# Layer norm of a convolution on one core: the mean over 1024 channels from one running sum and the last tile, in place of eight products

## The reference, cut to what matters

```python
def layernorm(x, g, b):
    mu = jnp.mean(xf, axis=-1, keepdims=True)
    var = jnp.mean(jnp.square(xf - mu), axis=-1, keepdims=True)
    y = (xf - mu) * lax.rsqrt(var + LN_EPS)
    return y * g + b

def conformer_conv(h, w_pw1, b_pw1, w_dw, b_dw, ln_g, ln_b, w_pw2, b_pw2):
    u = h @ w_pw1 + b_pw1
    a, gate = jnp.split(u, 2, axis=-1)
    u = a * jax.nn.sigmoid(gate)
    u = conv(u, w_dw, 31 taps, causal, one filter per channel) + b_dw
    u = jax.nn.silu(layernorm(u, ln_g, ln_b))
    return u @ w_pw2 + b_pw2
```

## Time and profile before

| | us |
|---|---|
| median of 3 runs (2274.26 to 2274.81) | 2274.33 |
| the profiled execution, its own time | 2274.24 |
| its span, first to last instruction | 2272.5 |
| TensorE busy | 2247.5 (99%) |
| VectorE busy | 1306.0 (57%) |
| ScalarE busy | 931.6 (41%) |
| GpSimd busy | 375.7 (17%) |
| the stage of the convolution, first tap product to the mean's last product | 816.7 to 988.9 |

### The profile page before, as it was taken

One profiled execution on the slowest core, in us unless ns is written; L12 is line 12 of the kernel. 1 busy time (PEld: TensorE's weight loads), 2 busy tenths in 40 slices (PEclk: granted clock), 3 DMA queues, 4 the chain that ended last, 5 costly groups with the idle time before them and its releaser, 6 DMA issues.

```text
span 2272.5 us, 32983 instructions
## 1 busy us (share of the span) xinstructions
PE 2247.5 (99%) x11012; PEld 1829.9 (81%) x11012; DVE 1306.0 (57%) x1848; ACT 931.6 (41%) x1438; POOL 375.7 (17%) x296
## 2 busy tenths in 40 slices
PE   8999999999999999999999999999999999999998
PEld 6777778888888898878888888887777888888886
DVE  5557756643434758875564544576665656454455
ACT  6675645442324544553332222254544333222222
POOL 2021101201010446723040000040000304000003
PEclk9999999999999999999999999999999999999999
DMA  4222223333333434412123333332121212333332
GB/s 145 65 66 62 69 74 102 111 93 94 100 99 115 120 101 131 131 46 84 56 85 101 93 100 95 95 95 66 56 65 56 84 56 87 99 93 102 96 96 87
DMA packets 395617, 202.80 MB, mean 89 GB/s; under 512 B 13792, under 2 KB 393200, under 8 KB 395520
## 3 DMA queue, kind: packets, MB, share of 16 engines
q1 hardware_dynamic: 394672, 199.34, 29.9%
q0 software_dynamic: 848, 2.16, 0.3%
HBM read 198.84 MB, written 2.10 MB: 88 GB/s over the span
## 4 chain that ended last, share of the span: by engine, by line
PE 87%; issue 6%; DVE 2%; ACT 2%; POOL 1%; DMA 1%; DVEq 0%; SPq 0%; ACTq 0%; POOLq 0%
PE bank L1816 24%; PE bank L1818 24%; PE bank L1817 24%; PE bank L2201 3%; PE bank L2193 2%; PE bank L1796 2%; PE bank L2290 1%; PE bank L2267 1%; PE bank L2363 1%; PE bank L2399 1%; PE bank L2110 1%; PE bank L2112 1%; PE bank L2111 1%; DVE m_w_lo L1148 1%; POOL m_sb_softplus L558 0%
## 5 line engine op out<-in xcount | busy, mean ns | idle before, releaser
L621 ACT ACTIVATE m_w_hi<-m_raw 128x1024 fp32r<-128x1024 f32 x332 | 351.3, 1058 | 823.4 <-PE bank L1818 819.6
L1816 PE MATMUL bank<-m_h_hi,m_w_hi 128*128 128x512 f32 x1504 | 608.2, 404 | 2.9 <-DVE m_w_lo L1148 1.6
L1818 PE MATMUL bank<-m_h_hi,m_w_lo 128*128 128x512 f32 x1504 | 587.0, 390 | 0.0
L1817 PE MATMUL bank<-m_h_lo,m_w_hi 128*128 128x512 f32 x1504 | 586.3, 390 | 0.0
L1148 DVE TENSOR_TENSOR m_w_lo<-m_raw,m_w_hi 128x1024 fp32r<-128x1024 f32 x332 | 447.8, 1349 | 108.5 <-ACT m_w_hi L621 105.0
L1816 PEld LDWEIGHTS bank<-m_h_hi,m_w_hi 128*128 128x128 f32 x1504 | 282.7, 188 | 66.7 <-issue 4.7
L1818 PEld LDWEIGHTS bank<-m_h_hi,m_w_lo 128*128 128x128 f32 x1504 | 282.3, 188 | 60.3
L1817 PEld LDWEIGHTS bank<-m_h_lo,m_w_hi 128*128 128x128 f32 x1504 | 282.9, 188 | 55.5 <-issue 2.4
L1816 PE MATMUL bank<-m_f_hi,m_w_hi 128*128 128x512 f32 x688 | 268.8, 391 | 0.2 <-DVE m_w_lo L1148 0.2
L1818 PE MATMUL bank<-m_f_hi,m_w_lo 128*128 128x512 f32 x688 | 267.8, 389 | 0.0
L1817 PE MATMUL bank<-m_f_lo,m_w_hi 128*128 128x512 f32 x688 | 267.7, 389 | 0.0
(11 more groups left out here) (394 smaller groups left out, 3064.5 us busy)
## 6 DMA issues: line engine op xcount, KB each, us to landing
m_raw<-in_ff_w SPq DMA_DIRECT2D x256, 256.0 KB, 3.0
m_raw<-in_conv_pw_w SPq DMA_DIRECT2D x48, 256.0 KB, 3.8
m_raw<-in_w_in SPq DMA_DIRECT2D x47, 256.0 KB, 3.2
m_raw<-in_w_ffn_gate SPq DMA_DIRECT2D x44, 256.0 KB, 3.1
m_raw<-in_w_ffn_up SPq DMA_DIRECT2D x44, 256.0 KB, 3.1
m_raw<-in_w_ffn_down SPq DMA_DIRECT2D x40, 256.0 KB, 2.9
m_raw<-in_w_gate SPq DMA_DIRECT2D x32, 256.0 KB, 3.0
m_mem_w<-in_mem_wk SPq DMA_DIRECT2D x32, 256.0 KB, 3.0
```

The lines of the kernel that those rows point to most:

```text
L621: act.activation(WH[:, v % 2], RAW[:, v % 2], ACT.Copy).then_inc(s.w_hi, 1)
L1816: pe.matmul(o, high[:, r, k, :], hi, start=start, stop=False)
L1817: pe.matmul(o, high[:, r, k, :], lo, start=False, stop=False)
L1818: last = pe.matmul(o, low[:, r, k, :], hi, start=False, stop=stop)
```

## The change

GpSimd gets a new buffer `TILE_SUM` (128x512, fp32) and six additions. Ahead of the tap sums of tile m, for m = 2 to 7, it adds finished tile m-1 to the running sum (the first of the six adds tiles 0 and 1); it waits for `cv_tile` to be m there. This stands in place of the wait for `cv_tile` to be m-1 that its first tap addition had. TensorE's eight mean products, six of them in the steps, one ahead of `last_taps` and one behind the last memory group, become two behind that group: one of `MEAN` with `TILE_SUM`, one with tile 7.

```diff
+        TILE_SUM = at("conv_tile_sum", 110, [P, T])
...
+            def tile_sum(m):
+                pool.wait_ge(s.cv_tile, m + 1)
+                total = pool.tensor_tensor(TILE_SUM[:], CV[:, 0, :] if m == 1 else TILE_SUM[:], CV[:, m, :], ALU.add)
+                if m == KD - 2:
+                    total.then_inc(s.cv_sum, 1)
+
             for m in range(KD):
                 total = SUMS[m % 2][:]
+                if m >= 2:
+                    tile_sum(m - 1)
                 for j in range(1, SUM_TAPS if m < KD - 1 else SUM_TAPS_LAST):
-                    if j == 1 and m >= 2:
-                        pool.wait_ge(s.cv_tile, m - 1)
...
-            def conv_mean(m):
-
-                pe.wait_ge(s.cv_tile, m + 1)
-                first, last = isinstance(m, int) and m == 0, isinstance(m, int) and m == KD - 1
-                return pe.matmul(TR[:], MEAN, pick(CV, m), start=first, stop=last)
+            def conv_mean():
+
+                pe.wait_ge(s.cv_sum, 1)
+                pe.matmul(TR[:], MEAN, TILE_SUM[:], start=True, stop=False)
+                pe.wait_ge(s.cv_tile, KD)
+                pe.matmul(TR[:], MEAN, CV[:, KD - 1, :], start=False, stop=True).then_inc(s.ln_mean, 1)
...
                 mem_value(0, 1, m, q + 1, SBK[2])
-                if before is not None:
-                    conv_mean(before)
                 mem_key(1, 2, m, q + 2, SBK[3])
...
             mem_value(1, 3, 1, 27, SBK[1])
             mem_value(1, 0, KD, 28, SBK[2])
-            conv_mean(KD - 2)
             last_taps()
             mem_value(1, 1, KD, 29, SBK[3])
-            conv_mean(KD - 1).then_inc(s.ln_mean, 1)
+            conv_mean()
```

More of the change, by code:

```diff
@@ L2217, in last_taps, with conv_units @@
                 mm.then_inc(s.cv_pe, 1)
-            def conv_units(m, prev=None, before=None):
+            def conv_units(m, prev=None):
                 if prev is None:
@@ L2238, in _ @@
             conv_units(1, 0)
-            conv_units(2, 1, 0)
+            conv_units(2, 1)
             with U.loop(pe, KD - 3, 2) as i:
-                conv_units(i + 3, i + 2, i + 1)
+                conv_units(i + 3, i + 2)
             mem_value(1, 3, 1, 27, SBK[1])
             mem_value(1, 0, KD, 28, SBK[2])
-            conv_mean(KD - 2)
             last_taps()
             mem_value(1, 1, KD, 29, SBK[3])
-            conv_mean(KD - 1).then_inc(s.ln_mean, 1)
+            conv_mean()
             for k in range(KD):
```

## The result

The changed kernel takes 2278.35 us (median of 16 runs, 2277.34 to 2279.82) against 2274.36 for the kernel before beside it (16 runs, 2274.01 to 2274.89). The ratio is 1.0018, with a 95% interval of 1.0010 to 1.0025: 4.0 us more, which is under the 0.2% that the prediction set as its bound for "same". The profiled execution took 2278.73 us, its span is 2277.0.

The account below looks back on a forecast made before the run. TensorE's queue was the bound, some 2 us behind a VectorE-ScalarE-GpSimd ring. Additions cost that ring 5.98, less 0.36 for a shorter wait; the last product then puts the subtraction 4.0 later: 2274.33 + 4.0 = 2278.3 us, range 2272.0 to 2280.0.

Parts of the forecast that it names:

- same: Whole kernel's time: a difference within 0.2%, 4.55 us, counts as no change; chance given 0.71.
- The bound: Convolution stage: TensorE's full queue ends last, some 2 us later than the closed loop of VectorE, ScalarE and GpSimd.
- the ring: Convolution steps: VectorE, ScalarE and GpSimd wait only for each other in a closed loop of 22.24 us a step.
- Part 1: TensorE's mean products, eight become two: 5.16 us leave its queue, of which 1.7 us can be had.
- Part 2: GpSimd's first tap addition in tiles 2 to 7 waits on one semaphore, not two: 0.36 us less.
- Part 3: GpSimd's six additions start beside VectorE's line 1542 (later 1549) and win, lengthening it: 5.98 us in sum.
- TensorE in time: End of the convolution stage: TensorE is ready for its last product, on tile 7, with 1.4 us to spare.
- the signs: TensorE's expected new waits: some 5 us ahead of the first memory group, some 1.4 ahead of taps and last product.
- the clock rival: TensorE, idle 5.9 us before the two memory groups, falls to 1.2 GHz there: 2282.2 us; chance 0.06.
- The subtraction: VectorE's subtraction behind the last mean product starts 4.0 us later, and the shift stays to the end.
- The first rival: VectorE's line 1542 wins the start against GpSimd's addition: 2.0 us less, 2272.3 us; chance 0.13.
- The whole gain arrives: The VectorE, ScalarE and GpSimd loop has unseen room, so all 5.16 us arrive: 2269.2 us; chance 0.03.

Follow-up runs that it names:

- two products alone: Changed kernel without GpSimd's six additions, old wait on the first tap addition, TensorE's first product reading tile 6 instead of the sum: 2274.5 us, ratio 0.9998.
- earlier split alone: Kernel before, with only ScalarE's twelfth tap product moved behind the second weight split, so that the split comes earlier: 2274.28 us, ratio 1.0000.
- both shortened: Changed kernel with GpSimd's tile addition waiting for the next input and ScalarE's twelfth tap product moved behind the second weight split: 2268.9 us, ratio 0.9976.
- the later addition: Changed kernel with GpSimd's tile addition waiting for the next tile's input (end of line 1549) instead of the finished tile: 2272.55 us, ratio 0.9993.
- the memset's kernel: Changed kernel with a GpSimd memset of the same 128x512 tile in the addition's place, same wait: 2274.19 us, ratio 0.9996.
- the additions alone: Kernel before plus GpSimd's six tile additions and their wait, with TensorE's eight mean products kept: 2281.15 us, ratio 1.0028.
- the second trace: Changed kernel, nothing altered, traced once more beside the kernel before: 2278.57 us, ratio 1.0020.
- the drain: Changed kernel with a drain of GpSimd's queue between the wait for the finished tile and the tile addition: 2274.21 us, ratio 1.0000.
- the fillers: Changed kernel with the tile addition waiting for the next input, plus two TensorE products nobody reads, put into its waits: 2272.34 us, ratio 0.9992.
- the split moved in the changed one: Changed kernel, addition still right behind the finished tile, with ScalarE's twelfth tap product moved behind the second weight split: 2275.33 us, ratio 1.0005.

## Why the prediction was right, point by point

**The bound.** Right: TensorE's queue and the ring through VectorE, ScalarE and GpSimd lay about 2 us apart at the end of the stage. With either shortened alone the other holds the time (two products alone: 1.5 us; earlier split alone: nothing), with both shortened all of it arrives.

**Part 1**, 1.7 of 5.16 us: measured 1.51 with the products alone and 1.70 with the later addition.

**Part 2**, 0.36 us from the shorter wait: about half came. The gap from first product to first addition did shrink as read: 906.03 to 907.45 with the later addition, 1.42, against 905.99 to 907.46, 1.47, with the products alone, which keep the old wait. What failed is the step "the additions are in the ring", taken to mean that each shortening arrives. Three additions later GpSimd meets VectorE's first weight split and stands still, here in the kernel with the later addition:

```profile
911.79 2.40 POOL L605 TENSOR_TENSOR m_tap_sum<-m_tap_sum,m_tap_product 128x512 f32<-128x512 f32 x1 [0.16 <-ACT m_tap_product L946]
911.83 1.22 DVE L1155 TENSOR_TENSOR m_w_lo<-m_raw,m_w_hi 128x1024 fp32r<-128x1024 f32 x1
```

The blocked addition ends 1.14 behind the split; at 844.46, with GpSimd 0.01 ahead instead of 0.04, 1.15. So its end hangs on the split and not on its own start, and an earlier start is swallowed. Only the step from tile 2 to tile 3 (22.62 against 22.70) and the sums of tile 7 (15.62 against 15.68) keep something of it. Together it is 149.50 against 149.69, **0.19** in place of 0.36 (the memset's kernel, with the new wait too, has 149.49); some 0.05 of that is scatter in the other steps.

**Part 3.** The start was taken as 904.87, 0.01 ahead of VectorE's; measured 0.01 to 0.02 ahead in five tiles. GpSimd as the winner, line 1549 at 1.81, the addition at 1.28: measured 1.80 to 1.83 and 1.27 to 1.29. Tile 3, with its idle gap: 0.68 predicted, 0.70 measured (1.45 against 0.75). The sum of 5.98 on the ring is what the additions alone show, 4.99 up to tile 7's line and 1.05 in it, 6.04.

**What the sum missed** in the changed kernel is smaller and goes the other way. In some steps a second collision turned over. In the kernel before, VectorE's first weight split and a tap addition start together, and VectorE wins each time. In the changed kernel GpSimd is 0.08 ahead at 915.30 and wins: the addition 1.27, line 1155 2.27. VectorE loses 1.06 there, but GpSimd's sums and ScalarE's second split come earlier, and VectorE's wait for that split shrinks from 2.70 to 1.28. Those steps are 22.98 and 23.01 instead of 23.28, some 0.3 less. Two steps did so in the first trace and three in the second, whose stage is 0.3 shorter. The kernels with the drain, with the fillers and with the split moved in the changed one have one each, 0.4 less. Here the shorter wait of Part 2 comes back: where VectorE isn't idle before this split, GpSimd is level with it at best under the old wait in tiles 2 to 6 (956.34 and 956.34 with the products alone), and under the new one 0.00 to 0.07 ahead where VectorE still wins. From 0.07 on GpSimd can win. That fits, and the runs' own spread (2277.3 to 2279.8, before 2274.0 to 2274.9) would fit too, but I traced only two executions of the changed kernel, so it isn't shown for the rest.

**TensorE in time.** Right: it waits ahead of the two groups, 5.28 and 4.88 where the signs had some 5 (the clock rival's own working gave 5.9), and it is ready for the last tile, by 1.04 and, in the second trace, by under 0.2 where 1.4 were expected. The wait of 1.4 ahead of the taps isn't there. The term that was off is the length of the two groups: no more than before was assumed, but they took 8.89 and 9.92, against 7.31. The stretch of 970 to 990 in the second trace (busy us by engine, granted clock, DMA share, GB/s):

```profile
970.00:990.00 20.00, 20.00 (x112) 15.68 (x111) 17.68 (x25) 5.88 (x10) 13.17 (x10) 0.90 0.09 27
```

So **the clock rival was half right**: an idle time of 5 us is followed by a granted clock of 0.90 over 970 to 990 (0.92 in the first trace). It didn't stay down for both groups: they lost 1.6 and 2.6 us, not 7.1, and the slack took it. With 2.6 lost almost nothing of the slack was left, so the point from which it decides, 2.8, stands.

**The subtraction**, +4.0: measured +3.6 and +3.3 by the traces, and +4.0 by the medians of the times. The prediction of 2278.3 against 2278.35 is therefore closer than its parts are, and that closeness is luck: the shorter wait was 0.2 too hopeful, the turned collision (about 0.3 a step) made it too gloomy, and what the medians have beyond the traces, 0.4 here and 1.2 in the second set (2278.57 against 2274.11, stage +3.3), fills the gap. That remainder stays open. How many steps turn, and how long the two groups run at the low clock, differ between the two traces and could make it.

**The first rival**, VectorE wins: refuted for the changed kernel, and its condition confirmed by the drain. 0.07 behind, GpSimd loses. Its price, 2.0 under before, was near: 150.28 is 0.9 under before's stage, with tile 3 lost, and the later addition's 149.50, with none lost, is 1.7. What it left out is the clock: it would have cost these kernels part of the gain in some runs, as the two groups of times show.

**The whole gain arrives**: refuted, for want of room in the second ring. The earlier split made the room.

## What to carry to other kernels

Before work is taken off the engine that fills the chain, compute the step of the next ring as well; the gain ends where they meet, here at 1.7 of 5.2 us, and only shortening both brings the rest. Work moved to GpSimd is not hidden because GpSimd is idle: what counts is whether a VectorE instruction with two SBUF inputs starts beside it, and a wait on a later semaphore can move the addition into the gap for nothing. Where an engine is freed, ask too whether it then idles with little work in between, since TensorE's next products may run at the lower clock.

## What the runs showed of the hardware

- **The recorded order of start does not name the winner below about 0.1 us.** `SCALAR_TENSOR_TENSOR` on VectorE lost when it started 0.05 ahead (180.99) and 0.01 behind (907.53), and won when it was 0.08 ahead (905.37). VectorE's `TENSOR_TENSOR` won when it was 0.01 behind the earlier trace rows and lost when it was 0.08 behind (915.38); 0.07 behind it won in the first trace of the changed kernel (961.36) and lost in the second (960.40). Read from the order of starts alone, one would have the winner wrong at 180.99 and at 844.47. It isn't the form alone that makes the offset: coming from an idle time of 1.73, the same `TENSOR_TENSOR` lost when only 0.03 behind (953.99 against 953.96, the kernel before with the split moved). What makes it, these runs don't tell.
- **The loser does most of its work after the winner's end.** Line 1549 lost 1.07 against an addition of 1.29 that started with it: it ended 0.55 after GpSimd, where its own length is 0.75. GpSimd's addition lost 0.54 against a VectorE instruction of 0.75: it ended 1.16 after VectorE (905.45), where its own length is 1.29. So the loss goes by the winner's length, and an earlier start of the loser is swallowed.
- **A write alone doesn't collide.** The memset of 0.53 beside line 1549 cost neither anything.
- **TensorE's clock falls after short waits too.** Two waits of 1.2 and 1.4 us with one product between them came before a fall in the trace with the later addition, and by its two groups of times in some of its executions and not in others, 1.4 to 1.6 us a time. There was none with 1.5 and 1.4 (drain), with 1.0 and 1.4 (changed kernel, first trace), or with 0.3 and 0.6 (fillers). In the kernel before, TensorE has the same 1.4 alone, behind full work, and the product after it takes 1.12.
